# Layer 1 of a two-layer mixture-of-experts backbone: each expert's down product placed behind the next expert's gate and up products

## What is computed

```python
combine = ...        # (tokens, 16): two experts of one group for each token, with their weights
out = jnp.zeros_like(t)
for e in range(N_EXPERTS):                      # 16
    h_e = jax.nn.silu(t @ w_gate[e]) * (t @ w_up[e])      # w_gate, w_up: 1024 x 512
    out = out + combine[:, e:e + 1] * (h_e @ w_down[e])   # w_down: 512 x 1024
x = x + g2 * out                                # last layer; a final rms_norm follows
```

## Time and profile before

| what | value |
|---|---|
| median of 3 runs | 1540.67 us |
| lowest and highest run | 1536.49 and 1540.75 us |
| span of the profiled execution | 1534.0 us |
| TensorE busy in it | 1411.7 us, 92% |
| VectorE, ScalarE, GpSimd busy | 906.6, 685.4 and 247.3 us |
| bytes read from HBM | 337.29 MB |
| experts of layer 1 | from 1287 to 1526 us of the span |
| transfers in 1312 to 1472 us | 419 GB/s, the 16 DMA engines busy all the time |

### The profile page before, as it was taken

The page is one execution under the profiler, slowest core; times in us unless marked ns, Lnnn a source line. Parts: engine busy times, 40 slices in busy tenths (PEclk is TensorE's granted clock), DMA queues, the critical chain, the costliest instruction groups (busy, mean ns, idle before and its releaser), DMA issues.

```text
span 1534.0 us, 17969 instructions
## 1 busy us (share of the span) xinstructions
PE 1411.7 (92%) x7076; PEld 977.7 (64%) x7076; DVE 906.6 (59%) x1200; ACT 685.4 (45%) x961; POOL 247.3 (16%) x211
## 2 busy tenths in 40 slices
PE   4999999998999976999999889989978997999997
PEld 1786567645888854777777568876837994343333
DVE  2567983855744446988888634976487763112112
ACT  2654452346233345777777446443336552101002
POOL 0006970600000001112110030084140000000000
PEclk9899999999999987999999959999989998999999
DMA  9611006793131535999999882111743755999990
GB/s 356 237 55 55 23 33 163 249 389 132 55 110 56 219 135 187 378 400 397 395 393 404 326 299 100 40 59 54 217 159 148 298 215 205 422 423 410 425 416 34
DMA packets 96461, 348.00 MB, mean 227 GB/s; under 512 B 21744, under 2 KB 22896, under 8 KB 84080
## 3 DMA queue, kind: packets, MB, share of 16 engines
q1 hardware_dynamic: 92704, 333.76, 57.2%
q0 software_dynamic: 2976, 10.49, 2.1%
q10 hardware_dynamic: 688, 2.49, 0.4%
HBM read 337.29 MB, written 9.44 MB: 226 GB/s over the span
## 4 chain that ended last, share of the span: by engine, by line
PE 51%; DVE 4%; ACT 2%; issue 2%; DMA 1%; POOL 1%; DVEq 0%; POOLq 0%
PE bank L1383 7%; PE bank L1405 4%; PE bank L1118 4%; PE bank L1115 4%; PE bank L1124 4%; PE bank L803 2%; PE bank L1144 2%; PE bank L1154 2%; PE bank L705 2%; PE bank L1149 2%; PE bank L1416 2%; PE bank L1362 1%; PE bank L761 1%; PE bank L941 1%; PE bank L943 1%
## 5 line engine op out<-in xcount | busy, mean ns | idle before, releaser
L2920 DVE TENSOR_TENSOR slab_lo<-slab,high 128x4096 fp32r<-128x4096 f32 x48 | 210.8, 4418 | 4.9 <-ACT high L2057 4.9
L2057 ACT ACTIVATE high<-slab 128x4096 fp32r<-128x4096 f32 x48 | 174.1, 3631 | 21.3 <-PE bank L1124 19.4
L2343 POOL DMA_INDIRECT feed_rows<-token_table,slot_token x16 | 44.9, 2805 | 475.2 <-DVE slot_token L2861 285.3
L1383 PE MATMUL bank<-narrow_slab,picked 128*64 128x512 f32 x256 | 112.5, 592 | 0.2 <-ACT picked L2223 0.2
L1384 PE MATMUL bank<-narrow_slab,picked 128*64 128x512 f32 x256 | 112.5, 592 | 0.0
L803 PE MATMUL bank<-hT,ring 128*128 128x512 f32 (+1 forms) x256 | 104.0, 545 | 0.0
L2212 ACT ACTIVATE gated<-bank 64x512 f32<-64x512 f32 x16 | 9.4, 589 | 166.6 <-PE bank L1384 166.6
L1383 PEld LDWEIGHTS bank<-narrow_slab,picked 128*64 128x64 f32 x256 | 35.0, 137 | 67.4 <-issue 66.9
L3085 DVE TENSOR_TENSOR hidden<-bank,gated 64x512 f32<-64x512 f32 x16 | 17.0, 1064 | 94.0 <-ACT gated L2212 94.0
L2300 POOL TENSOR_TENSOR pair<-pf 128x512 f32<-128x512 f32 (+1 forms) x32 | 34.4, 1076 | 223.3 <-DVE pb L2545 216.5
L1405 PE MATMUL bank<-narrow_slab,hiddenT 128*64 128x512 f32 x256 | 58.5, 597 | 11.2 <-issue 11.2
(11 more groups left out here) (413 smaller groups left out, 3208.3 us busy)
## 6 DMA issues: line engine op xcount, KB each, us to landing
ring<-in_w_ada SPq DMA_DIRECT2D x24, 2048.0 KB, 13.5
ring<-in_w_in SPq DMA_DIRECT2D x24, 2048.0 KB, 10.3
slab<-in_w_gate SPq DMA_DIRECT2D x16, 2048.0 KB, 14.2
slab<-in_w_up SPq DMA_DIRECT2D x16, 2048.0 KB, 14.6
slab<-in_w_down SPq DMA_DIRECT2D x16, 2048.0 KB, 14.9
narrow_slab<-in_w_gate SPq DMA_DIRECT2D x16, 2048.0 KB, 14.4
narrow_slab<-in_w_up SPq DMA_DIRECT2D x16, 2048.0 KB, 12.0
narrow_slab<-in_w_down SPq DMA_DIRECT2D x16, 2048.0 KB, 10.0
```

Source lines behind the costliest of these rows:

```text
L1383: T.matmul(bank[0][0:64, :], x, gate[:, k, :], start=(k == 0), stop=(k == KT - 1))
L2057: S.activation(half_of(e, kind)[:], w[:], ACT.Copy)\
L2343: G.indirect_dma_start(feed_rows[e % 2][0:DEALT, :], None, token_table, bass.IndirectOffsetOnAxis(ap=slot_token[0:DEALT, e:e + 1], axis=0))\
L2920: V.tensor_tensor(low[:], w[:], half_of(e, kind)[:].bitcast(f32), ALU.subtract)\
```

## The change

Only layer 1's first expert phase is touched. `LATE_ORDER` is the new order of the 48 products: gate 0, up 0, then for each e from 1 on gate e, up e, down e - 1, and last down 15. TensorE's list is rewritten to it: `into_hidden(e + 1)` stands right behind `turn_hidden(e)`, and `down(e)` comes after it. The loads are issued in the same order. Both halves of a gather stand together, behind the down product. A scatter half comes one expert later (at e - 3 in place of e - 2), and one more scatter half stands between the last transposes and the last down product. `turn_pairs` comes ahead of `turn_hidden`. On VectorE `keep_y(e - 1)` follows `make_hidden(e)`. ScalarE's list is the same. The number of products, copies and transfers is unchanged.

```diff
+    LATE_ORDER = [(0, GATE), (0, UP)]
+    for e in range(1, N_EXPERTS):
+        LATE_ORDER += [(e, GATE), (e, UP), (e - 1, DOWN)]
+    LATE_ORDER += [(N_EXPERTS - 1, DOWN)]
...
                         turn_pairs(None, 0)
+                        into_hidden(None, 0, 0)
                         for e in range(N_EXPERTS):
-                            into_hidden(None, e, e // 4 % 2)
+                            if e:
+                                down(None, e - 1)
                             if e + 4 < N_EXPERTS:
                                 ...
                                 pe.wait_ge(*total(ph, None, "cols_kept", e + 3, 1))
-                                gather_cols(None, e + 4, 2, (0,))
-                            if e > 1:
-                                p = e - 2 - e % 2
-                                scatter(None, p, p // 4 % 2, halves=(e % 2,))
-                            turn_hidden(None, e)
-                            if e + 4 < N_EXPERTS:
-                                gather_cols(None, e + 4, 2, (1,))
+                                gather_cols(None, e + 4, 2)
+                            if e > 2:
+                                p = e - 3 - (e - 3) % 2
+                                scatter(None, p, p // 4 % 2, halves=((e - 3) % 2,))
                             if e % 4 == 2 and e + 4 < N_EXPERTS:
                                 pe.wait_ge(*total(ph, None, "cols_kept", e + 4, 1))
                                 turn_pairs(None, e + 2)
-                            down(None, e)
+                            turn_hidden(None, e)
+                            if e + 1 < N_EXPERTS:
+                                into_hidden(None, e + 1, (e + 1) // 4 % 2)
+                        scatter(None, N_EXPERTS - 4, 1, halves=(1,))
+                        down(None, N_EXPERTS - 1)
...
-                            name, k = spent_by[l][(m - len(FIRST)) % 3]
-                            sp.wait_ge(*total(2, None, name, (m - len(FIRST)) // 3, k))
+                            e, kind = LATE_ORDER[m - len(FIRST)]
+                            name, k = spent_by[l][kind]
+                            sp.wait_ge(*total(2, None, name, e, k))
...
                             make_hidden(None, e)
+                            if e:
+                                keep_y(None, e - 1)
                             if e % 4 == 2 and e + 4 < N_EXPERTS:
                                 keep_spread(None, e + 2, (e // 4 + 1) % 2)
-                            keep_y(None, e)
+                        keep_y(None, N_EXPERTS - 1)
```

More of the change, by code:

```diff
@@ L350, in build @@
                     lane += range(SLOTS)
-                keys = [("moe", ph, e, k) for e in range(n) for k in range(3)]
+                keys = [("moe", ph, e, k) for e, k in (LATE_ORDER if ph == 2 else [(e, k) for e in range(n) for k in range(3)])]
                 loads += keys
@@ L1347, in weights @@
                     def weights(i, e, g):
-                        m = 3 * e + g
+                        m = LATE_ORDER.index((e, g)) if ph == 2 else 3 * e + g
                         turn = FIRST if ph == 2 else AGAIN
@@ L1490, in _ @@
                     for m in range(3 * phases[ph][1]):
-                        name, k = spent_by[l][m % 3]
-                        slot_spent[slot_of(("moe", ph, 0, 0)) + m] = total(ph, None, name, m // 3, k)
+                        e, kind = LATE_ORDER[m] if ph == 2 else (m // 3, m % 3)
+                        name, k = spent_by[l][kind]
+                        slot_spent[slot_of(("moe", ph, 0, 0)) + m] = total(ph, None, name, e, k)
                 if l == 0:
@@ L1535, in fill_first @@
             def fill_first(m):
-                at = FIRST[m % len(FIRST)]
-                sp.dma_start(narrow_slab[at][:].rearrange("p (k n) -> p k n", k=(KT, KT, 4)[m % 3]), flat[m % 3][N_EXPERTS + m // 3])\
+                at, (e, kind) = FIRST[m % len(FIRST)], LATE_ORDER[m]
+                sp.dma_start(narrow_slab[at][:].rearrange("p (k n) -> p k n", k=(KT, KT, 4)[kind]), flat[kind][N_EXPERTS + e])\
                     .then_inc(slot_full[at], 16)
```

## The result

| | before | changed |
|---|---|---|
| median of 4 runs, first chip | 1539.91 us | 1518.51 us |
| median, second chip (9 and 5 runs) | 1537.53 us | 1520.41 us |
| span of the profiled execution | 1534.0 us | 1515.0 us |
| start of the first gate matmul to start of the last down matmul of layer 1 | 232.4 us | 215.2 us |

The ratio is 0.987 (95% interval 0.9847 to 0.9893), and 0.9884 (0.9868 to 0.9899) where both kernels were timed again on another chip. That is 20 and 18 us, 1.3 and 1.2%; between the medians it is 21.4 and 17.1 us, so single us of the gain are not certain. The forecast was 1526.2 us with a range from 1520.5 to 1532.0. The sign was right, the size was not.

A forecast was written before the change was run, and what follows sets the result against it. TensorE was taken to bound the kernel, with transfers as full. Its own gain of 18.1 to 18.2 us, less 3.6 us waiting for up 15, gave -14.5 us: 1540.67 to 1526.2 us, range 1520.5 to 1532.0.

The forecast's parts named there:

- What bounds the kernel, and the wait named: Layer 1's experts: TensorE bounds, idle 1.01 us ahead of a down product while ScalarE copies gathered columns, then turned hidden.
- 1.28 us for each wait: Ahead of the down product: 1.75 us between starts against 0.47 without the wait, so each wait costs 1.28 us.
- TensorE's count: Layer 1's expert stage counted anew without the waits: 204.2 us, last down product at 1498.2, gain 16.6 to 18.2 us.
- the allowance of 1.6 us for the joints: Uncertainty for mistakes in the joints between kinds of matmul, 0.1 us for each of 16 experts.
- The two waits left in place: TensorE still waits 0.8 us ahead of expert 0's transposes and 0.7 us ahead of `turn_pairs` at expert 2.
- The loads' term: Weight loads from load 8 on land 5.0 us apart at best; up 15 lands at 1487.2, limiting the gain to 14.5 us.
- the wait of 3.6 us: Near the stage's end TensorE wants up 15 at 1483.7 but gets it at 1487.3, so it waits 3.6 us.
- The fast window of 431 GB/s: Fast end of the transfer windows: 4.87 us a load, up 15 lands at 1482.2, TensorE sets the end, gain 18.2 us.
- TensorE alone sets the end: Rival, chance 0.28: loads keep up, at a mean of 4.92 us or less; gain 16.6 to 18.2 us, 1523.3 us.
- Carrying to the median: Takes the 14.5 us gain from the median of the runs shown, 1540.67 us; span falls from 1534.0 to 1519.5.
- The clock: Rival, chance 0.06: waits for weights lower TensorE's clock, returning 2 to 3 us of the gain; 1529 us.
- Loads under way for 20 us or more: Sign in the profile after: loads take up to 20 us or more from issue to landing, in place of 10 to 15.

The follow-up runs named there:

- act_swap: The kernel before with two lines of ScalarE's list changed about, the turned hidden copied ahead of the gathered columns; ratio 0.9932.
- twenty raises: The changed kernel with at most two loads under way and SyncE raising an unused semaphore twenty times before each issue; load gap 5.7 us.
- four holes: Loads 20, 24, 28 and 32 issued only once the load ahead had landed: 1538.46 us in the kernel before, 1537.87 us in the changed kernel.

## Why the prediction was wrong, point by point

- **What bounds the kernel, and the wait named: right.** The idle 1.01 us was ScalarE's second copy behind the first one (`act_swap`). The prediction's 1.28 us for each wait is more than the wait: taking it away alone gave 1.10 us, and most of the rest is the gather standing in one piece.
- **TensorE's count: right.** The time from one down product to the next was to be 13.7 and is 13.69 us; without loads in the way the stage is 17.7 us shorter, in the range 16.6 to 18.2. Of the allowance of 1.6 us for the joints about 0.5 was needed. The two waits left in place are there, with 0.6 us for 0.8 and 0.7 for 0.7.
- **The loads' term: the step that failed.** "From there on 40 loads come one after another" at 5.0 us, "a faster TensorE ... makes the queue longer and the loads no earlier". They were earlier. The 419 GB/s of the earlier trace rows were not the rate of a full queue: in the kernel before, TensorE freed some buffers so late that the next load was issued 4.0 to 4.8 us ahead, and these loads cost more, 3 us or more in all. A faster TensorE frees them sooner and the rate rises to 428. With 4.93 us in place of 5.005 up 15 comes 37 x 0.075 = 2.8 us sooner, and the wait of 3.6 us would be 0.8; it was 0.5, since TensorE itself came a little later than counted. The DMA share of 1.00 misled me; it stays 0.99 at 410 GB/s and 0.96 at 370. The fast window of 431 GB/s stood in my own rows as an end of the range, and was the better value.
- **The rival that nearly came true** is "TensorE alone sets the end", with 0.28. Its turning point, 4.92 us a load, is where the kernel now stands: 0.5 us of wait in one profile, and one wait of 1.5 in the other, whose stage is 16.1 us shorter than before and not 17.2.
- **Carrying to the median: the second failure.** In the profiled pair the span fell by 19.0 us: 17.2 in the stage, and 1.8 because the stage began at 1285.1 and not 1287.0. That is scatter from the part ahead: over both kernels' variants the stage began at 1285.1 to 1291.6. I then took 6.7 us from the span to the median, 1540.67 - 1534.0, and it was 3.5 in the changed kernel. In the later runs the time is 1.7 to 1.9 us over the span of the same execution; the rest is how far the profiled execution, the fastest of its three, lay below the median. That can't be carried over from three runs: on the other chips the medians of the kernel before were 1537.53 (9 runs), 1537.88 (19) and 1540.57 (11). Of the 7.7 us between forecast and result 2.7 are the loads' term, 1.8 the earlier start, and 3.2 this. With the loads' term put right the forecast would have been 1523.5 us, still 5 us too slow. So the mechanism that failed is the loads', but what took the first result below the range was mostly scatter; 17.1 us, the difference of the medians in the second timing, taken from the same 1540.67, would lie within it.
- **The clock** stayed at 1.00 in 1312 to 1472. In the run with twenty raises, where TensorE waited up to 3.8 us for loads, it was 0.94 over that stretch, and with the four holes 0.98; the rival was real and its condition did not arise.
- **Loads under way for 20 us or more:** 28.1 us for up 15, as said. The last landing was to be near 1498 and was at 1492.2. Of these 6 us, 1.8 are the earlier start.

TensorE has about 1.3 us of waits left in the stage (experts 0 and 2). Taking them away should only lengthen the wait of 0.5 to 1.5 us for up 15, since nothing is left of the lead of the loads; that was not run.

## What to carry to other kernels

Before moving a product to hide a wait, look at what stands ahead of the awaited copy on its own engine: changing about two lines of ScalarE's list gave about 10 of the 18 us. A change that spends the lead of the transfers is worth its full count only as long as the lead lasts, so work out when the last load can land, and test the kernel with holes in the stream: here the same holes cost nothing that the timed runs show before, and 17 us after. Look too at when each load may be issued in the new order: one early load issued 0.1 us ahead made a hole of 2.8 us. Take the rate for such a sum from a stretch in which loads were issued well ahead, not from a mean with the DMA engines at a share of 1.00. And carry a gain to the median of the runs as a difference of times, not by the distance of one profile from a median of three.

## What the runs showed of the hardware

A stream of 2 MiB loads on one queue ran at 426 to 428 GB/s in 1312 to 1472 of the changed kernel, where each was issued 4.7 us or more ahead of the landing before it, with two under way as with six. Issued about 4.3 us ahead they ran at 410, and mostly 3.3 to 4.3 us ahead at 370 GB/s, with DMA shares of 0.99 and 0.96; the mean 16 KB packet took 0.635 and 0.681 us there against 0.616. A load issued only after the one ahead had landed came 7.8 to 8.8 us after it. From one down product to the next TensorE took 13.70 us at 428 GB/s and at 390.
